# Mixture-of-experts stage: experts ranked by their own tokens, in 128, 64 or 32 slots

## The reference, cut to what matters

```python
g_logits = (t @ w_rg) + b_rg                       # 4 groups of 8 experts
g_sel = jnp.argmax(softmax(g_logits), axis=-1)     # one group per token
e_logits = take_along_axis(einsum('td,dge->tge', t, w_re) + b_re, g_sel)
top_p, top_i = lax.top_k(softmax(e_logits), 2)     # two experts per token
combine = one_hot(8 * g_sel + top_i, 32) * g_p * top_p / sum(top_p)
for e in range(32):                                # t: 256 x 1024
    hid = jax.nn.silu(t @ w_gate[e]) * (t @ w_up[e])   # 256 x 256
    out = out + combine[:, e:e + 1] * (hid @ w_down[e])
```

## Time and profile before

| | |
|---|---|
| median of 3 runs | 1640.75 us |
| profiled execution, own time | 1638.27 us |
| its span in the trace | 1636.5 us |
| TensorE matmul busy | 1535.0 us (94%), 7240 matmuls |
| VectorE busy | 1177.8 us (72%) |
| ScalarE busy | 874.8 us (53%) |
| VectorE `w_lo` splits, whole kernel | 532 of 1249 ns mean |
| ScalarE `w_hi` splits, whole kernel | 532 of 1058 ns mean |
| HBM traffic | 198 GB/s over the span |

### The profile page before, as it was taken

The page is one execution under the profiler, slowest core; times in us unless marked ns, Lnnn a source line. Parts: engine busy times, 40 slices in busy tenths (PEclk is TensorE's granted clock), DMA queues, the critical chain, the costliest instruction groups (busy, mean ns, idle before and its releaser), DMA issues.

```text
span 1636.5 us, 19946 instructions
## 1 busy us (share of the span) xinstructions
PE 1535.0 (94%) x7240; PEld 1239.0 (76%) x7240; DVE 1177.8 (72%) x1528; ACT 874.8 (53%) x1129; POOL 135.2 (8%) x133
## 2 busy tenths in 40 slices
PE   7999999999998999999989999799977999999995
PEld 5787778888886787777868777678766888777774
DVE  5787677676776787676767777665556555899985
ACT  5644665544444644576444443446533445777872
POOL 0470000000000363000000000000000000000000
PEclk9999999999999999999999999899987999999998
DMA  7534334477666444333576766443205455899991
GB/s 298 180 129 155 129 132 152 171 281 282 251 240 237 160 155 154 130 131 127 180 282 246 267 234 247 152 155 107 100 13 206 160 184 186 305 350 345 347 363 47
DMA packets 45440, 326.06 MB, mean 199 GB/s; under 512 B 5280, under 2 KB 5280, under 8 KB 6688
## 3 DMA queue, kind: packets, MB, share of 16 engines
q1 hardware_dynamic: 38304, 278.94, 47.3%
q0 software_dynamic: 4608, 33.56, 5.3%
q10 hardware_dynamic: 2432, 12.30, 2.0%
HBM read 323.73 MB, written 1.05 MB: 198 GB/s over the span
## 4 chain that ended last, share of the span: by engine, by line
PE 49%; issue 30%; DVE 12%; ACT 6%; DMA 2%; POOL 0%; ACTq 0%; DVEq 0%; POOLq 0%
PE PS L147 47%; DVE PR L179 4%; DVE w_lo L168 2%; PE PS L152 2%; ACT w_hi L161 2%; DMA PR<-wada 2%; ACT S L161 1%; DVE PR L168 1%; ACT L161 1%; DVE S L168 1%; DVE h_lo L168 1%; DVE at_lo L168 1%; ACT PR L161 0%; ACT a_hi L161 0%; DVE S L179 0%
## 5 line engine op out<-in xcount | busy, mean ns | idle before, releaser
L168 DVE TENSOR_TENSOR w_lo<-stage,w_hi 128x1024 fp32r<-128x1024 f32 x532 | 659.2, 1249 | 310.9 <-ACT w_hi L161 305.8
L161 ACT ACTIVATE w_hi<-stage 128x1024 fp32r<-128x1024 f32 x532 | 559.9, 1058 | 556.9 <-PE PS L147 551.7
L147 PE MATMUL PS<-w_hi,a_hi 128*128 128x512 f32 x1088 | 437.1, 402 | 14.8 <-DVE w_lo L168 7.5
L147 PE MATMUL PS<-w_lo,a_hi 128*128 128x512 f32 x1088 | 425.4, 391 | 0.0
L147 PE MATMUL PS<-w_hi,a_lo 128*128 128x512 f32 x1088 | 425.2, 391 | 0.0
L147 PEld LDWEIGHTS PS<-w_hi,a_hi 128*128 128x128 f32 x1088 | 204.8, 188 | 66.1 <-issue 10.4
L147 PEld LDWEIGHTS PS<-w_hi,a_lo 128*128 128x128 f32 x1088 | 204.8, 188 | 44.3
L147 PEld LDWEIGHTS PS<-w_lo,a_hi 128*128 128x128 f32 x1088 | 205.1, 188 | 40.5 <-issue 1.0
L147 PE MATMUL PS<-w_hi,h_hi 128*128 128x512 f32 (+1 forms) x352 | 141.8, 403 | 6.6 <-issue 4.5
L147 PE MATMUL PS<-w_lo,h_hi 128*128 128x512 f32 (+1 forms) x352 | 138.5, 393 | 0.0
L147 PE MATMUL PS<-w_hi,h_lo 128*128 128x512 f32 (+1 forms) x352 | 137.9, 392 | 0.0
(11 more groups left out here) (240 smaller groups left out, 1645.3 us busy)
## 6 DMA issues: line engine op xcount, KB each, us to landing
stage<-wall SPq DMA_DIRECT2D x170, 1024.0 KB, 4.9
stage<-wexp SPq DMA_DIRECT2D x96, 1024.0 KB, 6.0
PR<-wada POOLq DMA_DIRECT2D x32, 1024.0 KB, 10.0
G<-gate_b ACTq DMA_DIRECT2D x2, 1536.0 KB, 8.6
G<-rows ACTq DMA_DIRECT2D x1, 2048.0 KB, 11.8
lsm<-small ACTq DMA_DIRECT2D x3, 563.0 KB, 3.6
X<-x_in ACTq DMA_DIRECT2D x1, 1024.0 KB, 5.0
PR<-rows ACTq DMA_DIRECT2D x1, 1024.0 KB, 4.9
```

What stands on the lines that cost most here:

```text
L147: ins = self.e.matmul(out, lhsT, rhs, start=start, stop=stop, skip_group_check=True)
L161: self.tell(self.e.activation(out, in_, func, **kw), sem, chain)
L168: self.tell(self.e.tensor_tensor(out, a, b, op), sem, chain)
```

## The change

Tokens are no longer sorted by group. On chip, the kernel counts the tokens of every expert and ranks the experts by that count. The last two experts of the list (30 and 31) are fixed: they come first and need no rank, so their weights can be fetched before the router is done. Then come the other 30 by rank. The first five experts (two fixed, three ranked) run on all 256 tokens in place, with `a_hi` and `a_lo` as they are, and add straight into the sums in banks 0 to 3. The next 4 have 128 slots, the next 8 have 64, the last 15 have 32.

An expert with fewer slots gathers its own tokens. The 30 - 3 = 27 experts form 6 packs of 256 slot columns (`PACKS`), each made in steps (`STEPS`): 8 steps "cols" (4 matmuls of 256 columns, then ScalarE and VectorE for hi and lo), 2 or 4 steps "rows" (two transposes of the one-hot matrix), one step "weights". There are 70 steps; 22 of them stand in experts 1 to 4, up to six each, the other 48 in experts 5 to 20, three each. The result of a block of 128 rows (one expert of 128 slots, or two experts of 64 or of 32) leaves banks 5 and 7 as `y_hi` and `y_lo` and is put into the sums by 8 matmuls (`block_sum_pe`): 16 blocks. Experts of 64 and 32 slots have hi and lo side by side as one stationary operand of 128 or 64 columns, so a gate and up product is two matmuls and not three; their product is copied out by ScalarE (`copied`) and turned and added up by 4 small matmuls into bank 4, the bank that the product itself uses.

Matmuls of 512 columns per expert: 72 with all tokens, 36 with 128 slots, 16 + 12 with 64, 16 + 8 with 32.

The core of the diff:

```diff
+FIXED, TOP_K = 2, 2
+WHOLE = FIXED + TOP_K * T // P - 1
+FIRST = {P: WHOLE, 64: FIXED + TOP_K * T // 64 - 1, 32: FIXED + TOP_K * T // 32 - 1}
+def steps_at(i, place):
+    if 1 <= i < WHOLE:
+        s = 6 * (i - 1) + place
+        return [s] if s < EARLY else []
+    s = EARLY + 3 * (i - WHOLE) + place // 2
+    return [s] if i >= WHOLE and place % 2 == 0 and s < len(STEPS) else []
...
+        def up_halves_pe(p, i):
+            c = slots_of(i)
+            for h in range(KD // 2):
+                if c:
+                    n, r = pack_of(i)
+                    p.wait_ge("pack_lo", KD * n + 2 * h + 2)
+                    if i > WHOLE:
+                        if slots_of(i - 1) == P:
+                            p.wait_ge("hid_lo", HID_BASE + i)
+                        else:
+                            p.wait_ge("ex_hid", hidden_before(i))
+                half_ready(p)
...
         def expert_down_pe(p, i):
+            if c:
+                p.wait_ge("y_lo", 2 * blocks_before(i))
...
         def experts_pe(p):
-            group_pe(p)
-            sort_first_pe(p)
-            expert_up_pe(p, 0)
+            narrow_pe(p, 3, 5)
+            up = up_halves_pe(p, 0)
+            next(up)
+            narrow_turn_pe(p, 3)
+            next(up)
+            next(up)
+            counts_pe(p)
+            next(up)
+            ranks_pe(p)
             for i in range(EXPERTS):
                 expert_turn_pe(p, i)
+                if i == 0:
+                    list_pe(p)
+                block_sums_pe(p, i, True)
+                steps_pe(p, i, 0)
                 if i + 1 < EXPERTS:
-                    expert_up_pe(p, i + 1)
+                    for h, _ in enumerate(up_halves_pe(p, i + 1)):
+                        if h < 3:
+                            steps_pe(p, i, h + 1)
+                block_sums_pe(p, i, False)
+                steps_pe(p, i, 4)
                 expert_down_pe(p, i)
...
         def experts_dve(v):
+            def columns(i):
+                ...
+                v.wait_ge("ex_silu", hidden_before(i + 1))
+                v.tt(slot_hid[:, 0:2 * c], sg[:, 0, 0:2 * c], PS[:, turn_bank(i), 2 * c:4 * c], ALU.mult, sem="ex_hid")
+                v.wait_ge("hid_hi", HID_BASE + i + 1)
+                v.tt(lo, ...)
...
             for i in range(EXPERTS):
+                columns(i)
+                steps_dve(v, i, 0)
                 if i + 1 < EXPERTS:
+                    for place in (1, 2, 3):
+                        spent_dve(v)
+                        steps_dve(v, i, place)
                     hidden(i + 1)
+                    spent_dve(v)
+                steps_dve(v, i, 4)
+                spent_dve(v)
+                steps_dve(v, i, 5)
+                spent_dve(v)
+                if i >= WHOLE and block_of(i)[2]:
+                    for nh, bank in enumerate(Y_BANKS):
+                        v.wait_ge("y_hi", 2 * blocks_before(i) + nh + 1)
+                        v.stt(y_lo[rows, cols], PS[rows, bank, :], row_weights[...], r32(y_hi[rows, cols]), ...)
```

More of the change, by code:

```diff
@@ L2188, in sort_first_pe @@
[L2188 to L2199, removed]
@@ L2263, in expert_down_pe @@
         def expert_down_pe(p, i):
-            tiles = [(h_hi[:, :, tok(t)], h_lo[:, :, tok(t)]) for t in range(len(group_of(i)))]
-            accs = [[PS[:, bank, :] for bank in sum_banks(x)] for x in group_of(i)]
+            c = slots_of(i)
             p.wait_ge("hid_hi", HID_BASE + i + 1)
             p.wait_ge("hid_lo", HID_BASE + i + 1)
-            if i >= PER_GROUP and i % PER_GROUP == 0:
-                p.wait_ge("y_hi", 2 * (i // PER_GROUP))
-                p.wait_ge("y_lo", 2 * (i // PER_GROUP))
+            if i == WHOLE:
+                p.wait_ge(*step_read(EARLY - 1))
@@ new lines, in expert_down_pe @@
+                todo = []
+                for t in range(tiles_of(i)):
+                    for nh in range(2):
+                        wh, wl = (w[:, slot, nh * W:(nh + 1) * W] for w in (w_hi, w_lo))
+                        if not c:
+                            out_, cols, first, last = PS[:, sum_bank(t, nh), :], tok(t), i == 0 and k == 0, False
+                        else:
+                            out_, cols = PS[:, Y_BANKS[nh], :], block_cols(i)
+                            first, last = k == 0 and not block_of(i)[1], k == 1
+                        hi, lo = h_hi[:, k, cols], h_lo[:, k, cols]
+                        if c == 32:
+                            todo += [(out_, hi, wh, first, False), (out_, hi, wl, False, last)]
+                        else:
+                            todo += [(out_, hi, wh, first, False), (out_, hi, wl, False, False), (out_, lo, wh, False, last)]
@@ new lines, in expert_down_pe, with sums_follow, block_sums_pe @@
+                for m, (out_, x, w, s0, s1) in enumerate(todo):
+                    p.mm(out_, x, w, s0, s1, sem="used" if m == len(todo) - 1 else None)
+                p.half += 1
+                if k == 0:
+                    steps_pe(p, i, 5)
+        def sums_follow(i):
+            return (i + 1, False) if slots_of(i) == P or i >= EXPERTS - 2 else (i + 2, True)
+        def block_sums_pe(p, i, turned):
+            for x in range(max(WHOLE, i - 2), i):
+                if block_of(x)[2] and sums_follow(x) == (i, turned):
+                    block_sum_pe(p, x)
```

595 lines of the change are left out of this document (372 added, 223 removed).

## The result

The changed kernel takes 1704.09 us (median of 4 runs, 1702.94 to 1707.59) and the kernel before 1640.2 (4 runs, 1639.04 to 1642.54): ratio 1.0397, 95% interval 1.038 to 1.0414. It is 64 us slower, in the direction forecast and inside the range (1640 to 1712), but 22 us above the forecast of 1682. The profiled execution's span is 1701.7 us; 1636.5 before.

The account below looks back on a forecast made before the run. In one-tile experts TensorE, VectorE and DMA were near their limit together. Turn 5, 128 slots, narrower experts, closing and clock: 1338.5 + 57 + 249 + 29 + 7 = 1680.5, plus 1.8: 1682 us; 8-in-10 range 1640 to 1712.

Parts of the forecast that it names:

- the new wait behind the turn: Next expert's product waits for VectorE's gated product or `h_lo`: 2.85 us after the turn, 4.45 us after a block.
- to turn 5: Opening and all-token experts 1 to 4: first turn at 1245, second 1266, turn 5 at 1338.5 us, before near 1348.
- 128 slots, 4 intervals: Intervals after turn 5: 12.2 us without a block, 15.5 twice after one, the fourth 13.7; together 57 us.
- 64 slots, 8: Eight intervals with steps: about 11.0 us, 12.5 after a block, mean 11.7; with one-hot set-up and a block's sum, 97 us.
- 32 slots with steps, 4: Four intervals of 32-slot experts with gathering steps beside them: 10.9 us each, 44 us.
- 32 slots without, 10: Last ten intervals: 9.6 us, 11.3 after a block, mean 10.8, 108 us; plus 7 us for cold TensorE, 1.4 five times.
- The wait of 4 us for the split of the fourth half: Opening, expert 1: small operations, `xs_lo` and one-hots stand before VectorE's split, so TensorE loses 4 us.
- 3 x 2.5 + 4 x 1.4: Possible half-clock cost of gaps after 128-slot and 64-slot blocks, 13 us; traces left it open, not in the sum.
- (a): Rival: the three engines overlap as now and only the busiest counts in late experts; 1616 us, faster; chance 0.12.
- (b): Rival: the chain behind the turn exists but is smaller, 29 us less over the late experts; 1653 us; chance 0.21.
- (c): Rival: TensorE stays at half clock through the late stage; 1738 us; chance 0.12 together with (d).
- (d): Rival: SyncE's reads of the rank delay the weights, shown as ScalarE waiting for the stage buffer; 1 in 50, within (c).

## Why the prediction was right, and 22 us short

The mechanism was right: the new wait behind the turn, the evictions in front of it, VectorE starved by the four slots, weights slower because nobody asks for them. The 22 us are those of the medians, 1704.1 for 1682; the stretches below account for 21 of them in the profiled execution. The terms:

| stretch | predicted us | measured us |
|---|---|---|
| to turn 5 | 1338.5 | 1344.8 |
| 128 slots, 4 intervals | 57 | 66.0 |
| 64 slots, 8 | 97 | 104.2 |
| 32 slots with steps, 4 | 44 | 48.2 |
| 32 slots without, 10 | 108 + 7 for the clock | 111.0 |
| last turn to the end | 29 | 27.4 |

*To turn 5, 6.3 us late.* The first turn is 2.5 us late (1247.5 for 1245). The interval behind it takes 20.5 us where 21 were forecast, but of other parts. A cold stretch was missed: TensorE waits 3.79 us for the first gated product, and most of the first half of expert 1 runs at half clock (1.6 us). The wait of 4 us for the split of the fourth half was put in too high: 0.96 us are measured, at the fifth half. The forecast had three halves ready at a turn; but TensorE is on none there, and all four slots can be full.

```profile
1247.51 0.90 PE L204 MATMUL PS<-csm,PR 128*128 128x128 f32 x3 [3.79 <-DVE PR L231]
...
1248.74 0.79 PE L199 MATMUL PS<-w_hi,a_hi 128*128 128x512 f32 x1
...
1249.34 0.63 PE L199 MATMUL PS<-w_lo,a_hi 128*128 128x512 f32 x1
1249.77 0.63 PE L199 MATMUL PS<-w_hi,a_lo 128*128 128x512 f32 x1
```

The next three intervals then take 20.6 to 20.8 us each where 19.8 was the sum, and the one to turn 5 takes 14.9 for 13; no run takes these apart.

*128 slots, 9 us short: the largest miss.* Here is the last interval, priced 13.7; it takes 17.5:

```profile
1393.35 0.38 PE L204 MATMUL PS<-csm,PR 128*128 128x128 f32 x2
...
1397.97 0.50 PE L199 MATMUL PS<-w_hi,pack 128*128 128x512 f32 x1 [4.01 <-DVE h_lo L220]
...
1399.01 0.63 PE L199 MATMUL PS<-w_hi,pack 128*128 128x512 f32 x1
...
1400.72 1.70 PE L199 MATMUL PS<-PR,onehot 128*128 128x2 f32 x8
...
1405.41 0.57 PE L199 MATMUL PS<-w_lo,pack 128*128 128x512 f32 x1
```

The chain up to the product was forecast right (4.45 us from the turn, 4.6 here), but TensorE was thought to stay at full clock. It doesn't: from 1399.0 to 1405.8 it runs at 1.2 GHz, 12 matmuls of 512 columns 0.2 us late each, 2.4 us. The "weights" step's small matmuls, 1.6 us at that clock and 0.9 at full, were in no term. The prediction had set aside 13 us for these gaps as open ("3 x 2.5 + 4 x 1.4"), because the earlier trace rows left open what lies between 2.47 and 3.47 us, and took them as nothing. That is the term which came out short. The rule of the Trainium skill ("TensorE: Matmul & The Clock Gate", "HAM oscillation"), that idle gaps once per loop make the burst behind them start cold, would have put the forecast at 1695. The trace agrees for the long gaps: all 14 of 2.6 to 4.1 us behind the turn after a block are followed by a stretch at half clock, at once or within 1.5 us, the 64- and 128-slot stretches standing at 0.93 and 0.87.

Shorter gaps do it too, but not always. In the first 128-slot interval, which has no block, the gap is 2.05 us:

```profile
1347.76 0.80 PE L199 MATMUL PS<-w_hi,pack 128*128 128x512 f32 x1 [2.05 <-DVE h_lo L220]
1348.35 0.63 PE L199 MATMUL PS<-w_lo,pack 128*128 128x512 f32 x1
...
1351.73 0.39 PE L199 MATMUL PS<-w_lo,pack 128*128 128x512 f32 x1
```

In the run with the opening moved the same gap at the same place leaves no slow matmul. The interval, with columns as above, first in the changed kernel and then in that run:

```profile
1344.80:1358.70 13.90, 11.85 (x51) 9.61 (x50) 8.08 (x11) 8.11 (x11) 0.00 (x0) 0.88 0.58 206
...
1344.10:1356.40 12.30, 10.25 (x52) 8.39 (x51) 8.09 (x11) 8.11 (x11) 0.00 (x0) 1.00 0.62 217
```

At full clock it takes the 12.2 us of the forecast; the half clock costs 1.5. The other three intervals can be held against the run with late evictions, where they stay at full clock: they are 3.3, 3.3 and 4.9 us longer here, 1.7 of it each time the longer gap, which leaves 1.6, 1.6 and 3.2 for the clock. Together 7.9 of the 9 us.

*64 slots and 32 with steps, 11.4 us short.* Three things are seen here: the same dips (0.93 and 0.89 in the rows), after gaps of 2.6 to 3.3 us; a turn by small matmuls that takes 0.8 us (64 slots) and 1.0 (32) up to the next matmul where 0.6 was taken (its bounds were 0.4 and 1.2), at most 3 us in 12 intervals; and steps that cost 14.5 us for the 11 taken, over 16 intervals. How the 11.4 us divide among them isn't shown. In the 64-slot stretch the clock can't be the most of it: with late evictions it is 8.8 us shorter, and four gaps shorter by 1.7 to 2.1 us are 7 of these.

*32 slots without steps.* 9.6 and 11.3 + 1.4 = 12.7 were the terms; 9.5 and 12.1 to 13.2 are measured, so the sum held. The 9.6 held by luck, as two errors in it cancel. The product comes 0.75 us later than forecast, since VectorE's row of `w_lo` ends 3.3 us behind the turn and not 2.5. And the last down half was thought to wait for three `w_lo`; it waits for two, because four halves are ready at the turn and not three. In the interval from 1620.38 the row of `w_lo` starts at 1626.32, two of them end at about 1628.6, and the last down half starts at 1628.82:

```profile
1626.32 5.77 DVE L220 TENSOR_TENSOR w_lo<-stage,w_hi 128x1024 fp32r<-128x1024 f32 x5 [1.83 <-ACT w_hi L213]
...
1628.82 0.47 PE L199 MATMUL PS<-w_hi,h_hi 128*128 128x512 f32 x1
```

*The rivals.* (a), overlap as before (1616), fell with the first interval. Its condition was that the three halves ahead bridge the turn: they don't, and not for one reason but for three, the bank, the evictions and the ring; with all three away ten late experts take 94.0 us for before's 89. (b), the smaller chain, would have had the ten late intervals in 99 us; they take 111, and the other stretches are longer than the forecast too. (c), half clock throughout (1738), holds for a part of most block intervals, never for a whole stage: 0.87 is the lowest stretch. (d) is refuted by the list of waits.

What stays open: why turns between 9 and 21 stay near 12 and 11 us an interval in the best version (95.4 us for 8 with 64 slots, VectorE busy 77.9 of them, and 43.4 us for 4 with 32). Gathering is 7.9 and 1.1 us of that; the rest isn't taken apart. Open is also how the last 5 us of the late stage divide between cold products and weights. No version run here is faster than the kernel before; the best complete ones are the 1668.5 of six slots and the 1670.6 of the evictions alone, which the runs don't tell apart.

## What to carry to other kernels

Before cutting an engine's work, read which other engines and queues are near their limit beside it: here VectorE's 8.05 us an expert bound the interval whatever TensorE did, so a draw was the most that fewer matmuls could reach there. When a change makes an operation wait for a result of the same step (a shared bank, an eviction in front), add up the whole loop through all engines, look for a second loop behind it (a ring of buffers), and expect them to hide each other: six slots gained nothing alone, and 6.7 to 8.5 us of late stage with the rest. Price a gap of TensorE by its length and by the slow matmuls behind it, and where the rows leave a gap length open, put half of the doubt into the sum instead of none.

## What the runs showed of the hardware that was not expected

The clock's fall doesn't follow the gap's length alone. In the experts' stages of these runs the gaps of 1.24 us left no mark, and those of 2.6 us and more before a product were each followed by a stretch at 1.2 GHz, at once or up to 1.5 us after the restart. Between them it went either way. A gap of 2.47 us left no mark in the first block; one of 2.05 us, behind 97 us of nearly full TensorE, left some 3.4 us at half clock, and left none at the same place when only the opening had been moved. Gaps of 2.40 and 2.01 us did the same in the runs with late evictions and with the filled gap. What tells them apart is open; neither the length nor the work just ahead of the gap does. So a price for a gap of 2 to 2.5 us is a chance times a cost, here of 1.5 us. After the gap of 4.01 us the first four matmuls still came 0.33 and 0.23 to 0.24 apart, and the fall to 0.43 came 1.0 us after the restart; after those of 4.1 us it was there at once, and lasted about 5 and about 3 us by turns, which is why the late block intervals take 13.2 and 12.1 us by turns. Four small fp32 matmuls (64 rows, 32 columns) take 1.0 us at full clock, shown as eight records: about as long as four 512-column ones (0.92).
